# Unnormalised inputs laid out by the host, per-token factors applied at the outcomes, and another order at the head of a two-layer hybrid block

## What is computed

```python
def rmsnorm(x, g):
    xf = x.astype(jnp.float32)
    y = xf * lax.rsqrt(jnp.mean(xf * xf, axis=-1, keepdims=True) + EPS)
    return (y * g.astype(jnp.float32)).astype(x.dtype)

def hybrid_layer(x, norm_g, w_in, ...):
    hn = rmsnorm(x, norm_g)
    z = jnp.einsum('bsd,de->bse', hn, w_in)
    (aq, ak, av, ag, mq, mk, mv, mo, mi, mf, mg, gq, gk, gv, ga, gg) = jnp.split(z, split_idx, axis=-1)
    att = band_chunk_attention(aq, ak, av, rel_bias);  y_a = att * silu(ag)
    qk = silu(causal_conv(concat([mq, mk]), conv_w))
    y_b = sigmoid(mo) * head_rmsnorm(mlstm(qk, mv, mi + b_i, mf + b_f)) * silu(mg)
    log_alpha = log_sigmoid(ga @ w_alpha + b_alpha) / GLA_TAU
    y_c = head_rmsnorm(gla(gq, gk, gv, log_alpha)) * silu(gg)
    return x + jnp.einsum('bse,ed->bsd', concat([y_a, y_b, y_c]), w_out)
```

## Time and profile before

| | us |
|---|---|
| median of three executions | 1566.72 |
| the profiled execution | 1568.99 |
| its span, first to last instruction | 1567.3 |
| PE busy in it | 1531.5 |
| DVE, ACT, POOL busy | 826.5, 721.6, 318.6 |

### The profile page before, as it was taken

One profiled execution on the slowest core, in us unless ns is written; L12 is line 12 of the kernel. 1 busy time (PEld: TensorE's weight loads), 2 busy tenths in 40 slices (PEclk: granted clock), 3 DMA queues, 4 the chain that ended last, 5 costly groups with the idle time before them and its releaser, 6 DMA issues. The chain is left out here.

```text
span 1567.3 us, 22091 instructions
## 1 busy us (share of the span) xinstructions
PE 1531.5 (98%) x8990; PEld 1294.3 (83%) x8990; DVE 826.5 (53%) x1412; ACT 721.6 (46%) x1404; POOL 318.6 (20%) x273
## 2 busy tenths in 40 slices
PE   7999999999999999999999999999999999999998
PEld 6888788998898887888888888678887888888887
DVE  5336656556445755845234443668956544244442
ACT  4335645465654644534124443567844443134431
POOL 1000142001430001344014431032001433024420
PEclk9999999999999999999999999989999999999999
DMA  7211112323220003333223332110012333223331
GB/s 245 68 58 64 55 54 89 129 68 108 83 93 28 28 1 108 92 97 121 93 81 95 99 111 86 37 45 15 15 67 81 102 100 120 82 81 98 114 101 51
DMA packets 37518, 127.99 MB, mean 82 GB/s; under 512 B 4248, under 2 KB 8872, under 8 KB 37416
## 3 DMA queue, kind: packets, MB, share of 16 engines
q1 hardware_dynamic: 37416, 126.57, 25.2%
HBM read 124.46 MB, written 2.10 MB: 81 GB/s over the span
## 5 line engine op out<-in xcount | busy, mean ns | idle before, releaser
L321 PE MATMUL bank<-hhi,whi 128*128 128x512 f32 x1056 | 415.8, 394 | 4.5 <-ACT hhi L1973 1.8
L323 PE MATMUL bank<-hhi,wlo 128*128 128x512 f32 x1056 | 411.8, 390 | 0.0
L322 PE MATMUL bank<-hlo,whi 128*128 128x512 f32 x1056 | 411.8, 390 | 0.0
L312 DVE TENSOR_TENSOR wlo<-wstage,whi 128x1024 fp32r<-128x1024 f32 (+10 forms) x250 | 278.4, 1116 | 110.2 <-ACT whi L302 109.9
L302 ACT CAST whi<-wstage 128x1024 fp32r<-128x1024 f32 (+10 forms) x250 | 236.0, 948 | 136.9 <-PE bank L323 131.9
L2458 DVE SCALAR_TENSOR_TENSOR cr<-bank,vc,cr 128x511 f32<-128x511 f32 (+1 forms) x168 | 125.8, 749 | 217.1 <-ACT cr L2397 214.1
L321 PEld LDWEIGHTS bank<-hhi,whi 128*128 128x128 f32 x1056 | 198.0, 188 | 50.6 <-ACT hhi L1973 4.2
L323 PEld LDWEIGHTS bank<-hhi,wlo 128*128 128x128 f32 x1056 | 198.0, 187 | 42.7
L322 PEld LDWEIGHTS bank<-hlo,whi 128*128 128x128 f32 x1056 | 198.1, 188 | 41.3 <-issue 0.5
L2397 ACT ACTIVATE cr<-bank,vc 128x512 f32<-128x512 f32 x84 | 65.5, 780 | 248.5 <-PE bank L323 248.5
L2503 POOL TENSOR_TENSOR cr<-cr,cr 128x512 f32<-128x512 f32 x44 | 94.2, 2140 | 315.6 <-DVE cr L2458 280.9
(11 more groups left out here) (418 smaller groups left out, 2308.9 us busy)
## 6 DMA issues: line engine op xcount, KB each, us to landing
wstage<-in_wts SPq DMA_DIRECT2D x147, 512.0 KB, 3.5
wstage<-in_wts SPq DMA_DIRECT2D x32, 704.0 KB, 4.1
wstage<-in_wts SPq DMA_DIRECT2D x12, 768.0 KB, 4.4
xT<-in_x SPq DMA_DIRECT2D x4, 512.0 KB, 4.9
xt<-in_x SPq DMA_DIRECT2D x4, 512.0 KB, 6.1
out<-ob SPq DMA_DIRECT2D x8, 256.0 KB, 2.3
U<-in_rel_ext SPq DMA_DIRECT2D x6, 256.0 KB, 9.1
wstage<-in_wts SPq DMA_DIRECT2D x2, 618.0 KB, 3.8
```

The costliest lines, as they stand in the source:

```text
L312: e.tensor_tensor(K.wlo[i % 3][:, p], K.stage[i % 3][:, p], K.whi[i % 3][:, p].bitcast(F32), SUB).then_inc(*K.dve.up(("wlo", i) if last el ...
L321: e.matmul(o, lh, rh, start=start, stop=False)
L322: e.matmul(o, lh, rl, start=False, stop=False)
L323: return e.matmul(o, ll, rh, start=False, stop=stop)
```

## The change

The host also gives x turned, as four pieces of two kt each (`x_turned`). SP's order becomes: chunk 0, turned piece 0, the constants, piece 1, chunk 1, pieces 2 and 3, token tiles 0 and 1, chunk 2, token tiles 2 and 3, chunk 3 (which waits for `wlo` of chunk 0), and then the bias and the small tensors as before. `hhi` and `hlo` are made from the turned x in SBUF, without the norm's factor; the turning on PE is gone. The squares are made at g = 3, the factors at g = 4, behind the splits of those steps; four matmuls spread the factors over the partitions (`rb`), behind ak0 on PE. ACT copies `rb` out at g = 5. Every outcome is multiplied by its factor: those with tokens on partitions by a per-partition scalar in the operation that reads them, those with tokens along the columns (aq, ak, mqk) by a new DVE operation `normed` into the single buffer `nt`, from which the split or the convolution goes on; gq goes from ACT to DVE. The four tiles of mv are computed in another order. The running maximum `Am` and its sum `FA` go behind the convolution of mqk4, and ACT's `em` behind the first tile of mo.

```diff
 def sp_init(e, q, K):
+    sp_load(e, q, K)
+    for j in range(4):
+        e.dma_start(K.xin[:, 2 * j:2 * j + 2, :], K.d["x_turned"][j]).then_inc(*K.turned_in[j].up(("xin", j), by=16))
+        if j == 0:
+            e.dma_start(K.vc[:], K.d["vecs"]).then_inc(*K.consts_in.up(by=16))
+            e.dma_start(K.fb[:], K.d["fox_b_f_2"].rearrange("a n -> n a")).then_inc(*K.consts_in.up("consts", by=16))
+        if j == 1:
+            sp_load(e, q, K)
     for c in range(4):
         e.dma_start(K.yt[:, c, :], x[:, c, :]).then_inc(*K.x_in[c].up(("x_in", c), by=16))
         if c == 1:
-            e.dma_start(K.vc[:], K.d["vecs"]).then_inc(*K.consts_in.up(by=16))
-            e.dma_start(K.fb[:], K.d["fox_b_f_2"].rearrange("a n -> n a")).then_inc(*K.consts_in.up("consts", by=16))
-    for _ in range(3):
-        sp_load(e, q, K)
+            sp_load(e, q, K)
+    sp_load(e, q, K)
 def act_x(e, q, K):
+    for kt in range(8):
+        q.wait_ge(*K.at(("xin", kt // 2)))
+        e.activation(K.hhi[:, kt, :], K.xin[:, kt, :], ACT.Identity, scale=K.col("norm_g", kt)).then_inc(
+            *K.act.up(("h1", "hi", kt)))
+def pe_factors(e, q, K):
+    b = K.RG.take(q, "rb")
+    q.wait_ge(*K.at("ident"))
+    q.wait_ge(*K.at("x_r"))
+    for c in range(4):
+        z = e.matmul(b[:, c * P:(c + 1) * P], factor(K, c).to_broadcast([P, P]), K.ident[:], start=True, stop=True)
+    z.then_inc(*K.pe.up("rb"))
 def pe_den(e, q, K):
     for key in (("aq", 0), ("ak", 0)):
         pe_fm(e, q, K, key, x, 8, T, K.RG)
+        if key[0] == "ak":
+            pe_factors(e, q, K)
         yield
...
-    for a in (0, 2):
-        for n, (part, c) in enumerate(((0, a), (1, a), (0, a + 1), (2, a), (1, a + 1), (2, a + 1))):
+    for row in (((0, 0), (1, 0), (0, 1), (2, 0)), ((1, 1), (2, 1)), ((0, 2), (1, 2), (2, 2)), ((0, 3), (1, 3), (2, 3))):
+        for part, c in row:
 def act_den(e, q, K):
     def conv(m):
         t = K.tmp.take(q, ("cv", m))
-        q.wait_ge(*K.at(("mqk", m)))
-        e.activation(t[:], K.bank(("mqk", m))[:], ACT.Identity, scale=K.col("conv_w", 4 * m + 3)).then_inc(
+        q.wait_ge(*K.at(("n", "mqk", m)))
+        e.activation(t[:], K.nt["n", "mqk", m][:], ACT.Identity, scale=K.col("conv_w", 4 * m + 3)).then_inc(
             *K.act.up(("cv", m, 0)))
-    yield
+    act_squares(e, q, K)
+    yield
+    act_factors(e, q, K)
+    yield
+    act_evac(e, q, K, "rfac", "rb", K.rb, K.bank("rb")[:])
     aqk(0)
     yield
     akk(0)
-    yield
     aqk(1)
     yield
...
-        if c % 2 == 1:
-            c -= 1
+        if c % 2 == 0:
             b = ("mv", 0, "c", c)
 def dve_den(e, q, K):
+    def normed(key, i, scale):
+        t = K.nt.take(q, ("n", key, i))
+        q.wait_ge(*K.at("rfac"))
+        q.wait_ge(*K.at((key, i)))
+        e.scalar_tensor_tensor(out=t[:], in0=K.bank((key, i))[:], scalar=scale, in1=K.rb, op0=MUL, op1=MUL).then_inc(
+            *K.dve.up(("n", key, i), frees=[(key, i)]))
+        return t
     def aqk(i):
-        dve_lo(e, q, K, ("aql", i), ("aq", i), ("aqh", i), K.aql[:, i, :], K.aqh[:, i, :], 0.125)
+        t = normed("aq", i, 0.125)
+        q.wait_ge(*K.at(("aqh", i)))
+        e.tensor_tensor(K.aql[:, i, :], t[:], K.aqh[:, i, :].bitcast(F32), SUB).then_inc(
+            *K.dve.up(("aql", i), frees=[("n", "aq", i)]))
...
+    conv(4)
+    conv_silu(1)
     q.wait_ge(*K.at("aj"))
     e.tensor_tensor_scan(K.Am, K.ones[0:6, 0:1].to_broadcast([6, T]), K.aj[0:6, :], 0.0, MUL, MAX).then_inc(*K.dve.up("Am"))
```

More of the change, by code:

```diff
@@ L536, in act_x, with dve_x, act_squares @@
 def act_x(e, q, K):
-    q.wait_ge(*K.at("epsc"))
+    yield
+    q.wait_ge(*K.at("consts"))
+    for kt in range(8):
[3 more added lines that the diff above has]
+    yield
+def dve_x(e, q, K):
+    yield
+    for kt in range(8):
+        q.wait_ge(*K.at(("h1", "hi", kt)))
+        e.scalar_tensor_tensor(out=K.hlo[:, kt, :], in0=K.xin[:, kt, :], scalar=K.col("norm_g", kt), in1=K.hhi[:, kt, :].bitcast(F32),
+                               op0=MUL, op1=SUB).then_inc(*K.dve.up(("h1", "lo", kt)))
+    yield
+def act_squares(e, q, K):
     for c in range(4):
@@ L542, in act_x, with act_factors, dve_squares @@
             *K.act.up(("x", "sq", c), frees=[("x", "junk", c)]))
[L543 to L553 removed]
+def act_factors(e, q, K):
+    q.wait_ge(*K.at("epsc"))
+    q.wait_ge(*K.at(("x", "sums")))
+    act_rstd(e, q, K, "x_r", K.small[:, 16:20], K.small[:, 16:20], D)
+def dve_squares(e, q, K):
     s = K.small
@@ L561, in dve_x, with dve_factors, factor, act_factor_evac @@
             *K.dve.up(("x", "sq2", c)))
[L562 to L575, removed]
+    q.wait_ge(*K.at(("x", "sq2", 3)))
+    q.wait_ge(*K.at(("x", "sq", 3)))
+    e.tensor_tensor(s[:, 16:20], s[:, 0:8:2], s[:, 1:8:2], ADD).then_inc(*K.dve.up(("x", "sums")))
+def dve_factors(e, q, K):
+    s = K.small
+    q.wait_ge(*K.at("x_r"))
+    e.tensor_scalar(s[:, 20:24], s[:, 16:20], -1.0, None, MUL).then_inc(*K.dve.up("x_nr"))
+def pe_factors(e, q, K):
+    b = K.RG.take(q, "rb")
     q.wait_ge(*K.at("ident"))
-    yield
-    banks = [(K.RA if kt < 7 else K.STAT).take(q, ("xT", kt)) for kt in range(8)]
+    q.wait_ge(*K.at("x_r"))
     for c in range(4):
[L580 to L585, removed]
+        z = e.matmul(b[:, c * P:(c + 1) * P], factor(K, c).to_broadcast([P, P]), K.ident[:], start=True, stop=True)
+    z.then_inc(*K.pe.up("rb"))
+def factor(K, c, sign=1):
+    return K.small[:, 16 + c:17 + c] if sign > 0 else K.small[:, 20 + c:21 + c]
+def act_factor_evac(e, q, K, name, bank, o, i, c):
+    q.wait_ge(*K.at("x_nr"))
+    q.wait_ge(*K.at(bank))
+    e.activation(o, i, ACT.Identity, scale=factor(K, c)).then_inc(*K.act.up(name, frees=[bank]))
+def dve_factor_evac(e, q, K, name, bank, o, i, c):
+    q.wait_ge(*K.at("x_nr"))
+    q.wait_ge(*K.at(bank))
+    e.tensor_scalar(o, i, factor(K, c), None, MUL).then_inc(*K.dve.up(name, frees=[bank]))
 def pe_den(e, q, K):
@@ L755, in act_den @@
         q.wait_ge(*K.at(b))
-        e.activation(K.G[:, c, :], K.bank(b)[:, 0:384], ACT.Exp, scale=-1.0).then_inc(*K.act.up(("mo", "exp", c), frees=[b]))
+        e.activation(K.G[:, c, :], K.bank(b)[:, 0:384], ACT.Exp, scale=factor(K, c, -1)).then_inc(
+            *K.act.up(("mo", "exp", c), frees=[b]))
         q.wait_ge(*K.at(("mo", "exp", c)))
@@ L903, in dve_den @@
         q.wait_ge(*K.at(("mg", "sig", c)))
-        e.tensor_tensor(K.G[:, c, :], K.bank(b)[:, 0:384], t, MUL).then_inc(*K.dve.up(("G0", c), frees=[b, ("mg", c)]))
+        e.scalar_tensor_tensor(out=K.G[:, c, :], in0=K.bank(b)[:, 0:384], scalar=factor(K, c), in1=t, op0=MUL, op1=MUL).then_inc(
+            *K.dve.up(("G0", c), frees=[b, ("mg", c)]))
         if c == 0:
@@ L907, in dve_den @@
         yield
+    q.wait_ge(*K.at(("att", "fin", 2)))
+    q.wait_ge(*K.at(("gqk", 0)))
+    e.scalar_tensor_tensor(out=K.gq[:], in0=K.bank(("gqk", 0))[:], scalar=32 ** -0.5, in1=K.rb, op0=MUL, op1=MUL).then_inc(
+        *K.dve.up("gq", frees=[("gqk", 0)]))
     yield
@@ L919, in dve_den @@
         q.wait_ge(*K.at((("ag", c), "sig")))
-        e.tensor_tensor(t, K.bank(b)[:, 0:384], t, MUL).then_inc(*K.dve.up(("ag", "silu", c), frees=[b]))
+        e.scalar_tensor_tensor(out=t, in0=K.bank(b)[:, 0:384], scalar=factor(K, c), in1=t, op0=MUL, op1=MUL).then_inc(
+            *K.dve.up(("ag", "silu", c), frees=[b]))
         yield
@@ L925, in dve_den @@
         q.wait_ge(*K.at((("gg", c), "sig")))
-        e.tensor_tensor(K.gg[:, c, :], K.bank(b)[:, 0:256], K.tmp["ggt", c][:, 0:256], MUL).then_inc(
-            *K.dve.up(("gg", "silu", c), frees=[b, ("ggt", c)]))
+        e.scalar_tensor_tensor(out=K.gg[:, c, :], in0=K.bank(b)[:, 0:256], scalar=factor(K, c), in1=K.tmp["ggt", c][:, 0:256],
+                               op0=MUL, op1=MUL).then_inc(*K.dve.up(("gg", "silu", c), frees=[b, ("ggt", c)]))
         yield
```

96 lines of the change are left out of this document (55 added, 41 removed).

## The result

The changed kernel is slower by 0.4%: 1573.12 us (median of 13 executions, 1569.62 to 1576.36) against 1567.32 us for the kernel before beside it (13 executions, 1562.54 to 1571.48). The ratio is 1.0038, with a 95% interval of 1.0026 to 1.0049: 5.8 us, where 4.5 had been forecast. The profiled execution took 1573.69 us, 4.70 more than the profiled one of before.

The account below looks back on a forecast made before the run. PE, busy 1531.5 of 1567.3 us, was taken as the bound. 1568.99 + 3.3 (head) - 0.3 (mv) + 1.2 (convolution) + 0.3 (rest) = 1573.5 profiled, median 1571.2; range 1562.5 to 1576.

Parts of the forecast that it names:

- The start and chunks 0 to 2: Head: loads at 1.3 us a tile, first product near 8 us, chunk 2 ending at 28.9 against 32.3 before.
- Chunk 4: Its load, behind the slow tail of the DMA queue, lands at 29.8 us; PE waits 4.4 us before av.
- The bound at the queue's best rate: At 416 GB/s through the tail as well, chunk 4 lands at about 27.0 us and 0.5 us are lost.
- Loss of the head: At av's second tile, whose bank waits for normed of aq1: 3.3 us lost, bounds 0.5 and 5.0.
- mv: Both mva waits go, chunk 11 is split later, PE waits 2.35 us at mqk0; net gain 0.3, bounds 0 and 1.0.
- The clock falls as before: Behind the 2.35 us wait at mqk0, PE's clock falls as it did behind the 1.68 us wait before.
- The convolution: ACT waits for normed: 0.4 us lost at mo and 0.8 at em; 1.2 lost in sum, bounds -0.5 and 2.5.
- the bound of -0.5: Convolution: the wait is spread enough for the clock to hold, 1.7 us back, so 0.5 us gained.
- The rest: mqk2 and mqk5 cost 0.3 us, bounds 0 and 1; everything after about 240 us is the same and only shifts.
- rival 3: Slower still: the clock falls once or twice more (bank wait in av, em), 1573 to 1577 us; chance 0.14.
- Rival 1: Queue drains well enough: chunk 4 at 27 to 28.5, head costs 0.5 to 2, 1567 to 1569.5 us; chance 0.27.
- Rival 2: Head even, waits at mqk0 and mo too short to drop the clock: 1562 to 1564 us; chance 0.17.

Follow-up runs that it names:

- before_mv: The kernel before with only the new order of mv's products and copies one step earlier: 1566.69 us beside 1567.32, ratio 1.0004 (0.9992 to 1.0016).
- padded pairs: The changed kernel with 24 unread transposes on PE ahead of the first product, against it without: 1570.60 us against 1573.89, and 1569.75 against 1573.17.
- both mends: The changed kernel with chunks 3 to 5 issued ahead of the bias and chunk 11 split in step 34: 1563.91 us beside 1567.18 for before, ratio 0.9979.

## Why the prediction was right, and where its steps were not

**The start and chunks 0 to 2.** Forecast: first product near 8 us; measured 8.36, and 8.01 and 7.83 in the other two. PE's wait for the factors was to be 1.1 us, it was 0.99 (0.23 and 1.02); chunk 2 was to start at 23.4, it started at 23.26. The pace of 1.3 us a tile, taken from the earlier trace rows, carried that far: the changed kernel moves 418 GB/s from 8 to 18 us. The Trainium skill ("DMA: Bandwidth & Descriptors", "Where 436 GB/s comes from") gives about 358 GB/s for a core's reads, and neither this trace nor that of before agrees. The same page of the Trainium skill, in its section of measurements, names about 358 GB/s as what each core gets when both of a pair stream. One core ran here, so no run shows that.

**Chunk 4.** Direction right, size somewhat too large. I had the whole tail behind the turned x and chunk 3 clear at 27.9 and the chunk land at 29.8; its cast, which waited for nothing else, started at 28.27, 29.03 and 29.49 in the three executions. The tail had been slow before (190 GB/s, 17 to 20 us), and I carried that slowness over. In the changed kernel the same small tensors stand in the queue with full weight tiles on both sides, and the windows show 387 GB/s from 18 to 23 us and 354 from 23 to 28. The bound at the queue's best rate was 27.0; the three lie between, two of them nearer to my value. The tail was held in another place as well: SP issued chunk 4 late (17.81 us), and no step of mine counted SP's own time. Wait ahead of av: 4.4 us forecast, 2.71, 3.74 and 4.10 measured in three executions. Loss of the head: 3.3 forecast (0.5 to 5.0), 1.5, 2.8 and 2.8 measured. So the term was oversized, by 0.5 to 1.8. The steps behind the landing held: split, wait, half clock, and `normed` of aq1 as the last one late, with the clock's price under the wait for the bank. The run with chunks 3 to 5 ahead shows the cause by taking it away: its 3.1 to 4.3 us are the 3.2 to 4.4 by which the head ends earlier.

**mv.** The wait was right to the size: 2.35 us forecast, 2.32 measured in five kernels (eight traces), padded ones and mended ones among them; the net of 0.3 lies inside the interval of before_mv. "The clock falls as before" was not: it fell behind this wait in five of the eight, and behind the old one in two of three, and in the profiled execution its absence made the row -1.9 where -0.3 was forecast. The wait was right because the prediction looked past the waits that were removed, to what would be late next.

**The convolution.** Right in kind, and in the profile's terms near: ACT's step at 134.6 (135.5), the next cast at 141.2 (142.2), `normed` holding the bank at mo (1.18 us of wait), em late by 0.20 where 0.8 was forecast, behind a tile at half clock (1.77 where the clock held). In the trace this part grew by 0.4 us only, where 1.2 and 0.3 for the other tiles were forecast. But the run that removes `normed` gained 4.1 us. Both hold: before had its own wait and fall of the clock here, which the change failed to remove. I had this as the bound of -0.5. So the forecast compared rightly with before, and it did not say what the better alternative was worth. Its doubt about the copy to SBUF was right, and more so than it said: a tap takes 742 to 749 ns from PSUM in before and 749 to 751 from SBUF in after, so not even the 0.2 us come back.

**The rest.** Forecast at nothing behind 240 us, which was wrong. The "issue" waits took 1.5 us in the profiled trace, 2.7 against the second trace of before, and 2.2 to 3.4 by the padded pairs. The last two of these hold falls of the clock too. The prediction does not name these waits, and they stand in the kernel before as well (2.3 us). No step of it asked what 24 records fewer in PE's list (32 turnings less, and 8 for the four spreading matmuls) do to everything behind.

**The sum.** 4.5 forecast, 5.8 measured, and the forecast's number owes something to luck: the head was oversized by 0.5 to 1.8, and the "issue" waits, which were left out, are of about that size. The median of 1573.12 lies at the upper edge of the forecast's own stretch (1569.5 to 1573), and just as well at the lower edge of rival 3's. Rival 1 (chunk 4 at 27 to 28.5) had the landing of the profiled execution but not of the other two, and its time (1567 to 1569.5) was wrong as it had no other cost beside the head. Rival 2 names the kernel that both mends make: a head ahead of before, no wait at mqk0. It was given 1562 to 1564, and came at 1563.9, but through two edits that were not in the change. Rival 3 (one or two falls of the clock more than in my sum, 1573 to 1577) is the one that I gave too little. My sum let the clock fall no oftener than before, save for one fall under the bank's wait; the executions lost 5.0 us more to it than those of before, about three pieces. One or two of these lie under the bank's wait, as forecast. The others have no term in the sum.

## What to carry to other kernels

An earlier start is worth what the last transfer of the head leaves of it: write down the landing times in the order of issue down to the first chunk that is needed behind the start, and put that chunk ahead of all that is needed later (two lines here, 3.1 to 4.3 us). When an order of products is changed so that an outcome comes earlier, look at which input buffer is thereby held longer: the last use of mv's first part moved by one step and its successor's split with it, which cost 4.5 to 5.4 us until it was undone. Where a fall of the clock costs 1.7 us in one execution and not in another, use traces to find the waits, and medians of a dozen executions and their mean granted clock to weigh them: a wait may cost more by the falls that it makes likely than by itself. And look whether a fall lies under another wait before counting it.

## What the hardware showed that was not expected

The lost clock comes in one size. Every fall in the 14 traces, save the one at the very end of each span, cost 1.71 us or a multiple (half the clock for 3.4 us or for twice or three times that). A wait of 1.0 to 2.9 us is not always followed by one: of two executions with a wait of 2.7 to 2.8 us ahead of av, one fell to 0.50 and one stayed at 1.00, and the wait of 2.32 us at step 37 was followed by one in five traces of eight.

PE waited for up to 2.85 us with no releaser in the profile, among the 32x32 matmuls of the linear attention, each time until 1.2 to 1.6 us after a 16 KB transfer on the instruction queue had landed. Adding 24 small matmuls 260 us earlier turned three such waits (4.4 to 4.8 us in all) into two (2.2 to 2.6, in one trace with a third of 0.34), and in the kernel before two (2.3) into three (3.6).

SP's own issues took longer with more in the queue: the six of the bias 3.07 us before, and 5.64 in the changed kernel, where the turned x and chunk 3 had been asked for ahead of them. Chunk 4 was issued the later for it.
